# Two projection units ahead of a phase border, query weights on another queue, one block fewer in a ring

## The reference, cut to what matters

```python
p = xn @ w_in                                     # xn = rms_norm(x)
o = concat(rms_norm(stick_breaking(...)), rms_norm(window_attention(...)))
h = x + o @ w_out
q = rms_norm(h) @ w_peer_q                        # 8 heads x 256
v1, i1 = top_k(q[:, 0] @ keys_1.T, 16); v2, i2 = top_k(q[:, 1] @ keys_2.T, 16)
best, pos = top_k(v1[..., :, None] + v2[..., None, :], 16)   # gives idx and gate
y = h + sum_k softmax(best)_k * gelu(u[idx_k] . xt) * v[idx_k]
```

## Time and profile before

| | us |
|---|---|
| median of 3 runs | 3078.54 (3074.54 to 3089.9) |
| profiled execution | 3078.77 |
| its span, first to last instruction | 3077.0 |
| mean granted TensorE clock | 0.907 of full |
| busy: PE, VectorE, ScalarE, POOL | 2464.4, 2211.9, 1411.0, 1523.5 |
| moved by DMA | 1216.86 MB, mean 395 GB/s |

### The profile page before, as it was taken

How to read it: one execution, slowest core, us unless ns; L and a number is a source line. 1 busy time by engine, 2 the same in 40 slices (tenths; PEclk the granted TensorE clock), 3 DMA queues, 4 the chain that set the end, 5 groups by cost and what they waited for, 6 DMA issues and landing times.

```text
span 3077.0 us, 44235 instructions
## 1 busy us (share of the span) xinstructions
PE 2464.4 (80%) x13294; PEld 1155.5 (38%) x13294; DVE 2211.9 (72%) x5717; ACT 1411.0 (46%) x3303; POOL 1523.5 (50%) x1597
## 2 busy tenths in 40 slices
PE   7978777787757887888878888788778877788777
PEld 4755334443324332433233333333343334432322
DVE  3278647684667867786778767886778767786886
ACT  2235323552237523763366436753676345653233
POOL 0034444444545556555655555555555555455553
PEclk8989989889979989999989998999889987889989
DMA  8369999899999999999999999999999999999997
GB/s 335 97 266 402 417 401 417 332 395 393 424 417 416 423 407 425 415 417 403 426 420 411 413 418 421 408 411 418 419 419 409 403 402 422 419 400 417 427 423 311
DMA packets 243631, 1216.86 MB, mean 395 GB/s; under 512 B 30528, under 2 KB 90304, under 8 KB 107200
## 3 DMA queue, kind: packets, MB, share of 16 engines
q0 software_dynamic: 152528, 1108.81, 87.1%
q1 hardware_dynamic: 90864, 105.22, 9.8%
HBM read 1197.56 MB, written 16.47 MB: 395 GB/s over the span
## 4 chain that ended last, share of the span: by engine, by line
DMA 34%; PE 25%; DVE 20%; issue 8%; DVEq 4%; ACT 3%; ACTq 2%; POOL 1%; SPq 0%; another core or an unknown queue 0%; POOLq 0%
DMA r_uv<-peer_uv,f_idx 30%; DVE r_uv L1216 8%; PE f_y_acc L1763 5%; PE f_z L1648 5%; PE f_y_acc L1744 3%; PE f_q_ps L1689 2%; DMA f_work<-scratch_projT 2%; PE f_y_acc L1615 2%; DMA f_work<-w_out 1%; PE f_z L1506 1%; POOL r_uv L996 1%; PE f_o_sw L1675 1%; ACTq L1140 1%; DVE f_ind L1357 1%; DVEq L1394 1%
## 5 line engine op out<-in xcount | busy, mean ns | idle before, releaser
L996 POOL DMA_INDIRECT r_uv<-peer_uv,f_idx x1056 | 1271.6, 1204 | 1186.5 <-PE f_y_acc L1763 817.4
L1216 DVE CUSTOM_DVE_ANT_0 r_uv<-r_uv,r_x_rep 128x1024 f32<-128x1024 f32 x1056 | 1290.9, 1228 | 551.4 <-DMA r_uv<-peer_uv,f_idx 526.0
L1763 PE MATMUL f_y_acc<-r_uv,f_diag 128*32 128x512 f32 x4224 | 676.0, 657 | 353.0 <-ACT f_diag L1142 344.7
L1136 ACT ACTIVATE f_act_hid<-f_hid 128x2 f32<-128x2 f32 x528 | 107.5, 204 | 1059.4 <-DVE f_hid L1216 1033.8
L1744 PE MATMUL f_y_acc<-r_neg_ones,f_zeros 128*32 128x512 f32 x948 | 454.3, 615 | 0.0
L982 POOL TENSOR_TENSOR f_gate_fold<-r_fold,f_gates 128x64 f32<-128x64 f32 x528 | 245.9, 466 | 282.6 <-ACT f_diag L1142 265.9
L1763 PEld LDWEIGHTS f_y_acc<-r_uv,f_diag 128*32 128x32 f32 x4224 | 104.9, 112 | 634.3 <-ACT f_diag L1142 515.1
L1689 PE MATMUL f_q_ps<-r_w_q,f_xnT 128*128 128x256 f32 x1152 | 313.6, 420 | 3.1 <-DVE f_pick L1348 3.1
L1142 ACT ACTIVATE f_diag<-f_gate_fold,f_act_hid 128x32 f32<-128x32 f32 x1056 | 281.9, 314 | 40.3 <-issue 4.4
L1689 PEld LDWEIGHTS f_q_ps<-r_w_q,f_xnT 128*128 128x128 f32 x1152 | 232.0, 209 | 117.6 <-issue 73.3
L1136 ACT ACT_TABLE_LOAD x210 | 269.4, 1283 | 3.8
(11 more groups left out here) (212 smaller groups left out, 3055.3 us busy)
## 6 DMA issues: line engine op xcount, KB each, us to landing
r_uv<-peer_uv,f_idx POOLq DMA_INDIRECT x1056
f_work<-scratch_projT SPq DMA_DIRECT2D x86, 128.0 KB
r_w_out<-w_blocks SPq DMA_DIRECT2D x36, 256.0 KB
f_work<-out_sb_v_prompt SPq DMA_DIRECT2D x72, 128.0 KB
r_uv<-w_blocks SPq DMA_DIRECT2D x16, 512.0 KB, 11.3
r_w_q<-w_peer_q SPq DMA_DIRECT2D x8, 1024.0 KB, 11.1
x_in<-x_prompt SPq DMA_DIRECT2D x8, 512.0 KB, 10.4
f_q_pad<-scratch_projT SPq DMA_DIRECT2D x64, 64.0 KB
```

Of the source, the lines that this page charges most:

```text
L996: pool.indirect_dma_start(uv[:, n % RING, :], None, io["peer_uv"], bass.IndirectOffsetOnAxis(ap=idx[:, head, k:k + 1], axis=0),).then_inc( ...
L1136: nc.scalar.activation(act_hid[:, batch % 4, :], hid[:, batch % 8, :], ACT.Gelu)
L1216: nc.vector.tensor_tensor_reduce(row_u, row_u, x_rep[:, g % 3, :], 1.0, 0.0, ALU.mult, ALU.add, hid[:, n // 2 % 8, n % 2:n % 2 + 1]).then_ ...
L1763: last = nc.tensor.matmul(y_acc[quarter, g % 2 * 512:(g % 2 + 1) * 512], diag[:, batch % 3, i, :], uv[:, n % RING, DM + b * 512:DM + (b + ...
```

## The change

Phase one ends with the first two middle units, projected into `y_acc`, which both phases now share, with its semaphore. For the banks, phase one's accumulators go from four to two. The chunks become 4, 4, 4, 3, 3 blocks; the last (blocks 15 to 17) lies in `x_rep` 0 to 2 instead of the ring and `x_rep` 0 and 1, so that ring place 7 holds one block instead of two, and gather 7 holds for 17 units instead of 18. The second half of `xnT_middle` moves from `x_rep` 2 to `g_final`. On ScalarE, VectorE and PE the order at the end of phase one changes: x 8 is normalised before the last chunk is copied.

`w_q` is no longer loaded in phase one but by ScalarE's queue, four pieces behind each of tile 0's two softplus. The first three `w_late` pieces are issued by SP in slot -23. The memset of `q_pad` and the first q loads are halved, and K of step 0 goes between the halves. The middle units move (each of the first eight units eight slots earlier, the others as listed), late units from slot 10 on start at 18 and are again where they were from slot 131 on.

```diff
-CHUNKS = ((4, 4), (0, 4), (8, 4), (12, 4), (16, 2))
+C_TRIPLE = 15
+CHUNKS = ((4, 4), (0, 4), (8, 4), (12, 3), (C_TRIPLE, 3))
...
-    r.xnT_middle = [half.rearrange("p (k t) -> p k t", k=DK // 2) for half in (r.y[:, 1, :], r.x_rep[:, 2, :])]
+    r.xnT_middle = [half.rearrange("p (k t) -> p k t", k=DK // 2) for half in (r.y[:, 1, :], r.g_final[:])]
     r.keys_in = r.y[:, 0, 0:2 * QH]
-    r.stage_last = r.y[:, 0, 2 * QH:2 * QH + P].rearrange("p (b t) -> p b t", b=1)
+    r.stage_last = r.y[:, 0, 2 * QH:2 * QH + 2 * P].rearrange("p (b t) -> p b t", b=2)
     r.w_ring = r.uv[:].rearrange("p r n -> p (r n)").rearrange("p (c k n) -> p c k n", c=2 * RING, k=DK)
-    r.w_pair = r.x_rep[:, 0:2, :].rearrange("p c (k n) -> p c k n", k=DK)
+    r.w_triple = r.x_rep[:].rearrange("p c (k n) -> p c k n", k=DK)
...
+    r.y_acc = ctx.enter_context(nc.psum_tensor("y_acc", [P, DM], F32))
+    r.s_late_mm = ctx.enter_context(nc.semaphore("late_mm"))
...
+MIDDLE_ORDER = [4, 5, 6, 7, 0, 1, 2, 3, 15, 16, 8, 9, 10, 11, 12, 13, 14, 17]
+BORDER_UNITS = 2
 LATE_ORDER = [0, 1, 2, 3, 4, 5, 6, 7, 8, 9, 10, 11, 17, 16, 12, 13, 14, 15]
 
 
-RING_PLACE = {**{c: c - 4 for c in range(4, 8)}, **{c: c + 4 for c in range(4)}, **{c: c for c in range(8, 16)}}
+RING_PLACE = {**{c: c - 4 for c in range(4, 8)}, **{c: c + 4 for c in range(4)}, **{c: c for c in range(8, C_TRIPLE)}}
...
-        squares = r.g_final
+        squares = r.w_late[:, 0:2, :, :].rearrange("p s k n -> p (s k n)")
...
-        acc = [ps(f"proj{s}", [P, 4 * P]) for s in range(4)]
+        acc = [ps(f"proj{s}", [P, 4 * P]) for s in range(2)]
...
-            def load_w_q(k):
-                sp.dma_start(r.w_q[:, k, :], io["w_peer_q"][k * P:(k + 1) * P, :]).then_inc(r.s_w_q, 16)
...
-                load_w_q(i - 4)
...
-            for k in range(len(ORDER) - 4, DK):
-                load_w_q(k)
-            for p in range(3):
-                load_late(sp, io, r, p)
...
-                nc.scalar.activation(rows[:, j, 0:n * P], acc[j % 4][:, 0:n * P], ACT.Copy,
-                                     scale=column_scale(c)).then_inc(s_ev, 1)
+                scaled = sum(column_scale(b) != 1 for b in range(c, c + n)) * P
+                if 0 < scaled < n * P:
+                    nc.scalar.activation(rows[:, j, 0:scaled], acc[j % 2][:, 0:scaled], ACT.Copy, scale=SCALE)
+                    last = nc.scalar.activation(rows[:, j, scaled:n * P], acc[j % 2][:, scaled:n * P], ACT.Copy)
+                else:
+                    last = nc.scalar.activation(rows[:, j, 0:n * P], acc[j % 2][:, 0:n * P], ACT.Copy, scale=column_scale(c))
+                last.then_inc(s_ev, 1)
...
             normalise(4)
+            normalise(5)
             rows_out(2)
-            normalise(5)
             normalise(6)
             rows_out(3)
             normalise(7)
+            normalise(8)
             rows_out(4)
-            normalise(8)
...
-            stage_out(1)
             scale_turned(3)
             normalise(5)
+            stage_out(1)
             scale_turned(4)
             normalise(6)
             scale_turned(5)
             normalise(7)
             scale_turned(6)
+            normalise(8)
+            scale_turned(7)
             stage_out(3)
-            scale_turned(7)
             stage_out(4)
-            normalise(8)
             scale_turned(8)
...
-                    if j >= 4:
-                        pe.wait_ge(s_ev, j - 3)
+                    if j >= 2:
+                        pe.wait_ge(s_ev, j - 1)
...
+            def middle_unit(u):
+                if u == 0:
+                    pe.wait_ge(s_xnT, T_LATE)
+                for k in range(DK):
+                    last = nc.tensor.matmul(r.y_acc[:, u * 512:u * 512 + MIDDLE], w_blocks_of(r, MIDDLE_ORDER[u], 1)[:, 0, k, :],
+                                            r.xnT_middle[k // 4][:, k % 4, :], start=(k == 0), stop=(k == DK - 1))
+                last.then_inc(r.s_late_mm, 1)
...
+            turn_x(3)
             project(2, 1)
             turn_rows(1)
-            turn_x(3)
+            turn_x(4)
             project(3, 0)
-            turn_x(4)
+            turn_x(5)
             project(3, 1)
-            turn_x(5)
+            turn_x(6)
             project(4, 0)
-            turn_x(6)
+            turn_x(7)
             project(4, 1)
             turn_rows(3)
-            turn_x(7)
             turn_rows(4)
             turn_x(8)
+            for u in range(BORDER_UNITS):
+                middle_unit(u)
...
-MIDDLE_ORDER = [4, 5, 6, 7, 0, 1, 2, 3, 17, 16, 8, 9, 10, 11, 12, 13, 14, 15]
 UNITS = [(c, "middle") for c in MIDDLE_ORDER] + [(c, half) for c in LATE_ORDER for half in range(2)]
 N_MIDDLE = len(MIDDLE_ORDER)
-MIDDLE_SLOT = [*(FIRST_SLOT + 8 + 4 * i for i in range(8)), -52, -47, -34, -30, -25, -19, -14, -8, 0, 5]
-LATE_SLOT = [*MIDDLE_SLOT, 10, 18, 22, 26, 32, 42, 50, 54, 58, 62, 66, 70, 76, 82, 87, 92, 100, 105, 109, 114, 131, 145, 155, 160,
-             165, 173, 177, 181, 185, 189, 193, 197, 201, 205, 209, 213]
+MIDDLE_SLOT = [*(FIRST_SLOT + 4 * i for i in range(8)), -60, -54, -47, -34, -28, -17, -11, -5, 1, 11]
+LATE_SLOT = [*MIDDLE_SLOT, 18, 26, 30, 34, 42, 50, 54, 58, 62, 66, 70, 74, 78, 82, 86, 90, 94, 102, 106, 114, 131, 145, 155,
+             160, 165, 173, 177, 181, 185, 189, 193, 197, 201, 205, 209, 213]
 BANKS = {"y": "y_acc", "Y": "y_acc2", "b": "o_sb", "w": "o_sw", "s": "sel_ps"}
-LATE_PLACE = [BANKS[a] for a in "yY" * 8 + "wb" + "sswswsswsbwbwbwbbwbwwsswbbwbsbwbwbwb"]
+LATE_PLACE = [BANKS[a] for a in "yY" * 8 + "wb" + "sswssswsbwbwbwbwbbwwwsswbbwbsbwbwbwb"]
...
-    for k in range(DK):
+    for k in range(DK) if u >= BORDER_UNITS else ():
...
-X_FIRST = [-10, -5, 12, 60, 98, 126, 168, 188]
+X_FIRST = [-10, -5, 20, 60, 98, 126, 168, 188]
...
-            hold(sync, S["zeroed"], 1)
...
-                for f in range(2):
-                    if t:
-                        hold(sync, S["zs"], 4 * t - 2 + 2 * f)
+                for f in range(2 if t else 1):
+                    hold(sync, S["zs"] if t else S["zeroed"], 4 * t - 2 + 2 * f if t else 1)
                     load_q(t, f, 2 * f)
+
+            def load_second_q():
+                hold(sync, S["zeroed"], 2)
+                load_q(0, 1, 2)
...
+                else:
+                    hold(sync, S["late_mm"], N_MIDDLE)
...
+                    if at == (0, 0):
+                        load_second_q()
...
+                if n == route_slot(0, 0):
+                    for p in range(3):
+                        load_late(sync, io, r, p)
...
-            nc.gpsimd.memset(q_pad[:], 0.0).then_inc(S["zeroed"], 1)
+            for f in range(2):
+                nc.gpsimd.memset(q_pad[:, f, :, :, :], 0.0).then_inc(S["zeroed"], 1)
...
-                    hold(pool, S["late_mm"], 2 * n + (2 if n < RING // 2 else 4))
+                    hold(pool, S["late_mm"], 2 * n + 2 if n < RING // 2 else min(2 * n + 4, N_MIDDLE - 1))
...
+            def load_w_q(e):
+                for k in range(e * DK // 2, (e + 1) * DK // 2):
+                    act.dma_start(w_q[:, k, :], io["w_peer_q"][k * P:(k + 1) * P, :]).then_inc(r.s_w_q, 16)
...
-                    act.wait_ge(S["late_mm"], N_MIDDLE if g == 2 else MIDDLE_ORDER.index(C_KVSW) + 1)
+                    act.wait_ge(S["late_mm"], MIDDLE_ORDER.index(C_TRIPLE + g) + 1)
...
                     softplus(*at)
+                    if at[0] == 0:
+                        load_w_q(at[1])
```

More of the change, by code:

```diff
@@ L180, in resident @@
     return r
+MIDDLE_ORDER = [4, 5, 6, 7, 0, 1, 2, 3, 15, 16, 8, 9, 10, 11, 12, 13, 14, 17]
+BORDER_UNITS = 2
 LATE_ORDER = [0, 1, 2, 3, 4, 5, 6, 7, 8, 9, 10, 11, 17, 16, 12, 13, 14, 15]
-RING_PLACE = {**{c: c - 4 for c in range(4, 8)}, **{c: c + 4 for c in range(4)}, **{c: c for c in range(8, 16)}}
+RING_PLACE = {**{c: c - 4 for c in range(4, 8)}, **{c: c + 4 for c in range(4)}, **{c: c for c in range(8, C_TRIPLE)}}
 def w_blocks_of(r, c, n):
-    if c >= C_KVSW:
-        return r.w_pair[:, c - C_KVSW:c - C_KVSW + n, :, :]
+    if c >= C_TRIPLE:
+        return r.w_triple[:, c - C_TRIPLE:c - C_TRIPLE + n, :, :]
     return r.w_ring[:, RING_PLACE[c]:RING_PLACE[c] + n, :, :]
@@ L247, in kept_blocks @@
         def kept_blocks(j):
-            return 1 if CHUNKS[j][0] == C_KVSW else CHUNKS[j][1]
+            return 2 if CHUNKS[j][0] == C_TRIPLE else CHUNKS[j][1]
         def stage_of(j):
-            return r.stage_last if CHUNKS[j][0] == C_KVSW else r.stage_first[:, TURNED.index(j), :, :]
+            return r.stage_last if CHUNKS[j][0] == C_TRIPLE else r.stage_first[:, TURNED.index(j), 0:CHUNKS[j][1], :]
         @block.sync
@@ L414, in project @@
                     pe.wait_ge(s_w[j], n * 16)
-                    if j >= 4:
-                        pe.wait_ge(s_ev, j - 3)
+                    if j >= 2:
+                        pe.wait_ge(s_ev, j - 1)
                 for k in range(4 * half, 4 * half + 4):
```

(11 more changed lines are left out.)

## The result

| | before | after |
|---|---|---|
| median, same sessions (6 runs each) | 3078.86 us | 3096.61 us (3089.23 to 3104.24) |
| ratio | | 1.0062, 95% interval 1.0044 to 1.0080 |
| profiled execution, span | 3078.77, 3077.0 us | 3093.02, 3091.2 us |
| mean granted TensorE clock | 0.907 | 0.906 |

The change makes the kernel 0.6% slower, where 3063 was forecast: 34 us off the median, beyond the range (3051 to 3075), on the side to which 0.07 was given.

What follows compares the result with a forecast made beforehand. From about 200 us DMA bytes over rate bound the time, so starting gap-free gathers sooner shortens the span. 1.4 + 4.7 + 2.0 + 8.4 - 1.0 = 15.5 us saved: forecast 3063 us, eight-in-ten range 3051 to 3075.

Steps and rivals of the forecast that it cites:

- w_q on the activation queue: Tile 0's windows: w_q's 8.4 MB share the engines with SP's small loads; charged 1.0 us, bounds 0 and 7.
- Rival (2): Tile 0's small loads stand behind w_q, dist up to 7 us late: 3070, up to 3075; chance 0.15.
- Moved and hidden: w_late loads moved to slot -23 and late units started 8 slots later cost 0; bounds -3 and +4 for the units.
- Rival (4): On SP's ordered queue, shifted late stores delay tile 1's and 2's key loads: 31 us, 3094 or more; chance 0.07.
- Start of the fused phase: Border of the phases: first scores at 68.1 instead of 69.5, 1.4 us saved, bounds 0 and 2.4.
- From scores to queries: Slots -85 to -23: PE does fewer pieces of units after the first scores, 4.7 us saved, bounds 3.5 and 6.4.
- Route to gather 0: Head 0's queries to gather 0: no unit in slots -22 to -18, 2.0 us saved, bounds 1 and 3.
- Gather 7: Before gather 7: holding for 17 units instead of 18 saves 8.4 us, bounds 0 and 9.4.
- rival 1: Border of the phases: PE's clock stays up, 5.7 us of half clock give back 2.9: 3060; chance 0.20.

Runs made afterwards that it cites:

- e1: Changed kernel with the late units' slots and banks of the kernel before, last middle unit at slot 5: 3075.89 us, ratio 1.0004.
- e7: e1 with w_q issued later by SP in eight single 1 MB pieces, instead of two bursts of four on ScalarE's queue: 3058.25 us, ratio 0.994.
- e6: Kernel before with only the changed kernel's late slots and banks, and the third early x copy at slot 20 instead of 12: 3096.02 us, ratio 1.0065.
- e9: e6 with the late slots behind slot 78 as in the kernel before, banks to match: 3085.81 us, ratio 1.004.
- e5: Kernel before with only w_q moved, from phase one to two bursts of four on ScalarE's queue: 3082.69 us, ratio 1.0027.
- e2: Changed kernel with w_q loaded again in phase one on SP's queue, all else as changed: 3081.71 us, ratio 1.0019.
- e3: Changed kernel with both undone: w_q in phase one again and late units as in the kernel before: 3059.4 us, ratio 0.9953.
- e8: e3 with gather 7 holding for all 18 middle units instead of 17: 3072.88 us, ratio 0.9997.

## Why the prediction was wrong, step by step

Wrong in sign by two terms of the sum.

- **"w_q on the activation queue", charged 1.0 us (bounds 0 and 7): it cost 15.3** (e1 against e7, gather 0), above the upper bound. The step that failed is "half of the rate for 1 MB is 5 us, and 5.4 for the load". The queues shared packets and not bytes: with one packet each in turn, SP's queue got 6 to 10% of the rate (0.03 MB of 0.48 in 86.7 to 88 us), not half, while its own 1 MB of w_first and its small transfers stood ahead of the value window. The value window landed after 19.2 us instead of within 6. The evidence for fair shares was weak: the 5.4 and 10.4 are of loads of 64 and 512 KB. And by its own terms the step gives 5 + 5.4 - 6.0 of slack = 4.4, not 1.0. Rival (2) named this mechanism and put it at 7 to 12 us of loss with a chance of 0.15: right place, too small. The cover that I claimed for ScalarE, 3.92 us for a first batch of 2 to 4, was used up by a batch of 7.19.
- The Trainium skill's rule from "DMA: Bandwidth & Descriptors", "Queues, rings and completion order", is that an engine takes turns between queues packet by packet. The trace agrees with it (68 and 69 packets, 96 and 96, 110 and 110). What I drew from it did not follow: a small load waits for packets, but for one large packet of the other queue with each packet that stands ahead of it on its own, and 64 KB took 19.2 us beside the burst and 1.9 us without it. The skill's sentence against the move, in "Issuing engines are not separate DMA queues" (a second issuing engine saves only the time to issue), agrees as well: 414 GB/s on two queues over 87 to 106 us, 412 on SP's alone in e7 over 100 to 110.
- **"Moved and hidden", late units entered at 0 (bounds -3 and +4): they cost 19.1** (e6) to 20.7 us (e1). I looked at whether PE's order had room and whether DMA was full anyway, and not at what each unit waits for: three buffers of w_late, two of which come free only with the block's second unit, behind which the load then takes up to 20 to 25 us in a full stretch. The list before had 4, 6, 8, 4, 4, 6, 5, 8, 4 slots for that, the new one 4, 8, 4, 4, 4, 4, 4, 4, 4. Fewer slots are part of it; the longest wait comes at a distance of 4 that both lists have, but with no other wait to cover it (e9). Rival (4), the only slower one, was of the right size (31 us lost, 3094) and the wrong place: not stores ahead of key loads, but late w_late. That the result lies near its 3094 is luck. Its chance of 0.07 was too low because I had asked only about SP's order.
- **Start of the fused phase, 1.4: measured 0** (69.57 and 69.60), within its bounds. PE ends the two units at 64.4, the phase opens 2.0 later than before where I had 0.8, and my sum was short by 0.3 (63.7 + 0.95 + 1.3 + 0.55 is 66.5, not 66.2). What w_q's leaving gives depends on the rest: 1.8 in the kernel before (e5), but 4.4 beside the two units at the border (73.98 in e2, 69.60 after); without it the border units would have cost 4.4. The memset and load split did what was said; the turn ahead of the scores, which waits 2.03 us for ScalarE's eviction, was not in my order.
- **From scores to queries, 4.7: 5.3** once the burst is out (e7: first scores at 69.82, queries at 139.75, 69.9 us; before 144.82 - 69.57 = 75.2). **Route to gather 0, 2.0: 1.9** (160.27 - 139.75 = 20.5, before 22.4). Both right, though some 1 us of the first is the clock's (next but one).
- **Gather 7, 8.4 (upper bound 9.4): 13.5 against the trace of before, but 8.9 for the hold** (e3, e8), as worked out. Of the other 4.6 some 3 are the idle ScalarE and the low clock in the one trace of before: there the first experts batch comes 21.4 us behind gather 0 (188.62), in e5, e6 and e9, with the same unit slots, 15.8, and in e7 15.3 (175.58 - 160.27). So the term was right, and I had taken its "old clock" from a row that a repetition doesn't show.
- **The clock (rival 1)** came half true: it stayed up to about 69 us, 0.91 over 60 to 80 against 0.62, but the scores at 69.60 still took 2.04 us for four records. It was low (0.50) for some 3 us of PE's work instead of 5.7. From the first scores to the second it is 6.0 us after and 6.3 in e7 against 7.25 before, so it gave 1.0 to 1.2 us. In e1 the clock fell sooner (0.51 over 68 to 70), and there it gave nothing (7.4).

Without the two failed terms the sum would have been 0 + 5.3 + 1.9 + 13.5 = 20.7: e7's gather 7 is 20.4 sooner. With 10.5 for gather 7, against the mean of e5, e6 and e9 (29.5) instead of the one trace, it is 17.7; the median moved 18.6 (3076.9 - 3058.25), against 15.5 forecast. With the two terms, 17.7 - 15.3 - 20 = 17.6 slower; the medians are 17.8 apart.

## What to carry to other kernels

A transfer moved from a full stretch into an emptier one must be checked against the small loads that are then in the air. As queues take turns by packet, a queue of small packets beside one of large packets gets few of the bytes: count the packets that stand ahead of the small load on its own queue, and give each the time of a large one. The same 8.4 MB cost 15 us as two bursts ahead of the small loads and nothing as eight single pieces behind them. Whether the pieces or the order did it is open. A list of units squeezed to catch up is not free because its engine has room: take the time (not only the slots) between the use that frees a buffer and the use that needs it refilled, and compare it with the landing time of that stretch. A part of a change that "only shifts things back" deserves its own term; here it was worth more than the whole gain forecast. And a row that a forecast leans on should be looked for in a second execution: here the one trace had a stall of 3 us that the same code doesn't show elsewhere.
